# Two transformer blocks on one core: the embedding stage ends tile by tile, and block 2 opens without a row norm stage

## What is computed

```python
def first_block(x, p, ...):
    for i in range(DEPTH):
        h = rms_norm(x, g_mix[i])
        ...
        x = x + merged @ w_out[i]
        x = x + expert_choice_moe(rms_norm(x, g_moe[i]), ...)
        ple_gate = jax.nn.sigmoid(rms_norm(x, g_ple[i]) @ w_ple_gate[i])
        x = x + ple_gate * (p[i] @ w_ple[i])
    return rms_norm(x, g_final)

def second_block(x, c, norm_g, w_ada, ...):
    for l in range(DEPTH):
        h = hybrid_layer(h, c_silu, cos, sin, norm_g[l], ...)
    return rms_norm_2(h, final_g)
```

## Time and profile before

| | us |
|---|---|
| median of 3 runs (3681.97 to 3682.17) | 3681.98 |
| the profiled execution's own time | 3682.63 |
| its span, first to last instruction | 3680.9 |
| PE busy in the span | 3421.2 (93%) |
| DVE busy | 1760.2 (48%) |
| ACT busy | 1064.4 (29%) |
| POOL busy | 38.6 (1%) |

### The profile page before, as it was taken

How to read it: one execution, slowest core, us unless ns; L and a number is a source line. 1 busy time by engine, 2 the same in 40 slices (tenths; PEclk the granted TensorE clock), 3 DMA queues, 4 the chain that set the end, 5 groups by cost and what they waited for, 6 DMA issues and landing times. The chain is left out here.

```text
span 3680.9 us, 41926 instructions
## 1 busy us (share of the span) xinstructions
PE 3421.2 (93%) x16364; PEld 2281.5 (62%) x16364; DVE 1760.2 (48%) x3023; ACT 1064.4 (29%) x1684; POOL 38.6 (1%) x42
## 2 busy tenths in 40 slices
PE   7999996999988999996999997999999999999999
PEld 5866673444446866675444445777766687777666
DVE  7766633212135875744121224467654355666443
ACT  4343322101023334322011013343333234433322
POOL 1000000000000200000000000000000000000000
PEclk9999998999998999997999998999999999999999
DMA  5521127999963441124999982212321331222213
GB/s 191 193 94 58 58 86 310 423 423 424 424 250 129 157 144 58 58 94 189 420 424 424 423 351 71 93 61 66 92 81 69 106 115 58 68 76 86 69 69 115
DMA packets 129376, 653.28 MB, mean 177 GB/s; under 512 B 22036, under 2 KB 32276, under 8 KB 62136
## 3 DMA queue, kind: packets, MB, share of 16 engines
q1 hardware_dynamic: 129208, 650.98, 45.6%
HBM read 632.54 MB, written 14.72 MB: 176 GB/s over the span
## 5 line engine op out<-in xcount | busy, mean ns | idle before, releaser
L1733 PE MATMUL ps<-normed_T_hi,ring_split 128*128 128x512 f32 x1920 | 609.8, 399 | 7.5 <-PEq L264 7.5
L1733 PEld LDWEIGHTS ps<-normed_T_hi,ring_split 128*128 128x128 f32 x1920 | 354.5, 188 | 107.4 <-issue 34.3
L1733 PE MATMUL ps<-normed_T_lo,ring_split 128*128 128x512 f32 (+1 forms) x960 | 376.1, 392 | 0.0
L2486 PE MATMUL ps<-normed_T_hi,ring_split 128*128 128x512 f32 x1024 | 336.1, 410 | 8.9 <-DVE branches L2752 7.6
L2065 DVE TENSOR_TENSOR ring_split<-weight_ring,ring_split 128x2048 fp32r<-128x2048 f32 x76 | 174.0, 2289 | 151.9 <-ACT ring_split L1921 151.6
L2486 PEld LDWEIGHTS ps<-normed_T_hi,ring_split 128*128 128x128 f32 x1024 | 192.9, 192 | 81.6 <-issue 32.7
L1733 PEld LDWEIGHTS ps<-normed_T_lo,ring_split 128*128 128x128 f32 (+1 forms) x960 | 180.2, 188 | 40.0
L2486 PE MATMUL ps<-normed_T_lo,ring_split 128*128 128x512 f32 x512 | 202.6, 396 | 0.0
L1789 PE MATMUL ps<-branches 128*128 128x512 f32 x384 | 173.0, 593 | 3.3 <-issue 3.0
L1230 PE MATMUL ps<-weight_ring,projected 128*64 128x512 f32 x768 | 167.9, 593 | 0.0
L1921 ACT ACTIVATE ring_split<-weight_ring 128x2048 fp32r<-128x2048 f32 x76 | 144.9, 1912 | 52.5 <-DMA weight_ring<-in_w_slabs 48.1
(11 more groups left out here) (443 smaller groups left out, 6028.3 us busy)
## 6 DMA issues: line engine op xcount, KB each, us to landing
weight_ring<-in_w_slabs SPq DMA_DIRECT2D x78, 1024.0 KB, 4.9
weight_ring<-in_w_exp_gate SPq DMA_DIRECT2D x48, 1024.0 KB, 16.9
weight_ring<-in_w_exp_down SPq DMA_DIRECT2D x48, 1024.0 KB, 12.2
weight_ring<-in_w_exp_up SPq DMA_DIRECT2D x48, 1024.0 KB, 20.5
weight_ring<-in_w_branch_gate SPq DMA_DIRECT2D x32, 1024.0 KB, 4.9
spare_weights<-in_w_exp_up SPq DMA_DIRECT2D x32, 1024.0 KB, 21.0
spare_weights<-in_w_exp_gate SPq DMA_DIRECT2D x32, 1024.0 KB, 20.3
spare_weights<-in_w_exp_down SPq DMA_DIRECT2D x32, 1024.0 KB, 15.7
```

Source lines behind the costliest of these rows:

```text
L1733: ins = e.matmul(dst, lhs(k, m), rhs(k, m), start=k == 0 and m == 0, stop=k == KD - 1 and m == 2)
L2486: ins = e.matmul(dst, lhs(k, m), rhs(k, m), start=k == 0 and m == 0, stop=k == KD - 1 and m == 2)
```

## The change

In `embedding_stage`, PE now does kh = 0 of tile 0, then the side products, then kh = 1 of tile 0, and for tiles 1 to 3 both halves of the depth one after the other; so tiles end one by one. ACT adds up the squares of each finished tile there (`squares`), and in the last layer DVE also writes `gained_X` = `X` times the gain of `g_final`, and ACT adds up its squares too. SP loads the first slab of the next stage in this stage, and ACT and DVE split it ahead of the stage that uses it. The norm stage ahead of layer 1's front (`summed`) then has no squares, no load and no split of slab 0. `row_norm_stage` and the norm stage behind it are gone: both roots come from the two sums (the second norm's variance is m2/(v+eps)+eps, with m2 the mean square of the gained row, which is worked out as eps*(v+eps)+m2 for the product of both roots). `layer2_stage(0)` is called with "summed" and opens by itself: four small DVE operations, one root, one reciprocal, three tiles scaled by DVE and one by ACT, 32 transposes, and steps 0 and 1 in halves of 256 tokens. POOL writes the normed `X` itself, four tiles of 128x1024; SP saves each tile to DRAM when POOL has written it, and SP and DVE wait for the four stores before they go on.

```diff
-        def norm_stage(loads, scale_col, bias_col=None, experts_of=None, save=False, slabs=None, ple=None):
+        def norm_stage(loads, scale_col, bias_col=None, experts_of=None, save=False, slabs=None, ple=None, summed=False):
...
-                        for q in range(3):
+                        for q in range(int(summed), 3):
...
+                    if summed:
+                        e.tensor_tensor(sums[:, 3, 0:1], sums[:, 3, 0:1], sums[:, 4, 0:1], ALU.add).then_inc(s["vector_step"], st.add("vector_step"))
+                        e.wait_ge(s[st.name], st.value)
+                        e.tensor_scalar(var, sums[:, 0:4, 0], 1.0 / D, EPS, ALU.mult, ALU.add).then_inc(s["var_ready"], 1)
...
 def embedding_stage(l):
...
                 @block.sync
...
+                            if last_layer:
+                                e.dma_start(rope_T[:, :, :], a["c_rope_T"]).then_inc(s["inputs_loaded"], 16)
+                                e.dma_start(gain_row, a["g_final"].partition_broadcast(P)).then_inc(s["inputs_loaded"], 16)
+                                e.dma_start(small[:, 136:152], modulation_saved[0, :, :]).then_inc(s["inputs_loaded"], 16)
+                    e.wait_ge(s["lo_ready"], 2)
+                    e.dma_start(ring_land[:, 0, :], next_slab).then_inc(slot_loaded[0], 16)
...
                 @block.tensor
...
+                    e.wait_ge(s["lo_ready"], 2)
+                    e.wait_ge(s["exp_done"], 1)
+                    exact_products(e, PS[:, 0, :], 0, 0, 0, 512)
+                    e.wait_ge(s["side_landed"], 16)
+                    for t in range(NT):
+                        e.wait_ge(s["gate_used"], t + 1)
+                        for k in range(2):
+                            ins = e.matmul(PS[:, 4 + t, :], p_T[:, k, t * P:(t + 1) * P], ple_side[:, k, :], start=k == 0, stop=k == 1)
+                        ins.then_inc(s["side_ready"], 1)
+                    e.wait_ge(s["lo_ready"], 3)
+                    for t in range(NT):
+                        if t:
+                            exact_products(e, PS[:, t, :], t, 0, 0, 512)
+                        exact_products(e, PS[:, t, :], t, 1, 1, 512).then_inc(s["product_ready"], 1)
...
                 @block.scalar
...
+                    e.wait_ge(slot_loaded[0], EXPERT_LOADS + 32)
+                    e.wait_ge(s["lo_ready"], 3)
+                    e.activation(ring_hi[:, 0, :], ring_land[:, 0, :], ACT.Copy).then_inc(s["slab_hi"], 1)
+                    sigmoid(1, 0)
+                    squares(0, 0, whole, 5, 1)
+                    sigmoid(1, 1)
+                    squares(1, 1, whole, 6, 2)
+                    squares(3, 4, low, 4, 3)
+                    sigmoid(1, 2)
+                    squares(2, 2, whole, 7, 4)
+                    sigmoid(1, 3)
+                    e.preload_act_table(ACT.Sqrt)
+                    squares(3, 3, high, 8, 5)
...
-        def layer2_stage(l, turned_by_last):
+        def layer2_stage(l, begun):
...
                 @block.sync
...
+                        for q in (1, 2):
+                            e.dma_start(ring_land[:, q, :], a["w_slabs_2"][l, q, :, :]).then_inc(slot_loaded[q], 16)
+                        for t in range(NT):
+                            e.wait_ge(s["pool_ready"], t + 1)
+                            e.dma_start(x_saved[t * P:(t + 1) * P, :], X[:, t, :]).then_inc(s["stored"], 16)
+                    e.wait_ge(s["stored"], 16 if half_turned else 64)
...
                 @block.tensor
...
+                        e.wait_ge(s["scaled_by_vector"], 1)
+                        turn_tile(e, s, U, open_banks, 0, lambda pair: None)
+                        e.wait_ge(s["scaled_by_scalar"], 1)
+                        turn_tile(e, s, U, open_banks, 1, None)
+                        e.wait_ge(s["scaled_by_vector"], 2)
+                        turn_tile(e, s, U, open_banks, 2, lambda pair: e.wait_ge(s["turned_taken_scalar"], 2 * pair - 2) if pair >= 2 else None)
+                        e.wait_ge(s["scaled_by_vector"], 3)
+                        turn_tile(e, s, U, open_banks, 3, None)
+                        half_step(0, 0, lambda k: k + 1)
+                        half_step(1, 0, lambda k: 8)
+                        half_step(0, 1, lambda k: k + 9)
+                        half_step(1, 1, lambda k: 16)
...
+                @block.gpsimd
...
+                        e.wait_ge(s["rstd_ready"], 1)
+                        for t in range(NT):
+                            e.tensor_scalar(X[:, t, :], gained_X[:, t, :], open_rstd[:, t:t + 1], None, ALU.mult).then_inc(s["pool_ready"], 1)
...
                 @block.scalar
...
+                        e.activation(U[:, 1, :], gained_X[:, 1, :], ACT.Copy, scale=open_rstd[:, 5:6]).then_inc(s["scaled_by_scalar"], 1)
+                        take_turned(e, s, open_banks, 0, 2, range(KD), lambda k: 0)
+                        take_turned(e, s, open_banks, 1, 4, range(KD), lambda k: k + 1)
...
                 @block.vector
...
+                        for t in (0, 2, 3):
+                            e.tensor_scalar(U[:, t, :], gained_X[:, t, :], open_rstd[:, 4 + t:5 + t], None, ALU.mult).then_inc(s["scaled_by_vector"], 1)
+                        split_taken(e, s, 0, range(KD), 0, st_)
+                        split_taken(e, s, 1, range(KD), 8, st_)
+                        e.wait_ge(s["stored"], 64)
...
-        row_norm_stage("g_final")
-        norm_stage([(modulation_cols, modulation_saved[0, :, :])], scale_col2, shift_col, save=True, slabs=lambda q: a["w_slabs_2"][0, q, :, :])
         for l in range(DEPTH):
-            layer2_stage(l, l > 0)
+            layer2_stage(l, "half turned" if l else "summed")
```

More of the change, by code:

```diff
@@ L1047, in _, with gain @@
+                    def gain(t, cols, done):
+                        if last_layer:
+                            e.wait_ge(tile_done, done)
+                            e.tensor_tensor(gained_X[:, t, cols], X[:, t, cols], gain_row[:, cols], ALU.mult).then_inc(gained, 1)
                     split(1, 1)
                     split(2, 0)
-                    add(0)
+                    for t in range(NT):
+                        add(0, t)
                     split(3, 1)
-                    add(1)
@@ L1052, in _ @@
[L1052 removed]
+                    e.wait_ge(s["slab_hi"], 1)
+                    e.tensor_tensor(ring_lo[:, 0, :], ring_land[:, 0, :], ring_hi[:, 0, :].bitcast(F32), ALU.subtract).then_inc(s["slab_lo"], 1)
+                    if last_layer:
+                        e.wait_ge(s["inputs_loaded"], 48)
+                    add(1, 0)
+                    gain(0, whole, 5)
+                    add(1, 1)
+                    gain(1, whole, 6)
+                    gain(3, low, 4)
@@ L1055, in mixer_kernel @@
+                    add(1, 2)
+                    gain(2, whole, 7)
+                    add(1, 3)
+                    gain(3, high, 8)
+                    e.wait_ge(tile_done, 8)
         chosen = T[:, 3072:3584].rearrange("p (t n) -> p t n", t=NT)
@@ L1325, in mixer_kernel @@
         half_var = small[:, 16:17]
+        open_var, open_root, open_rstd = (small[:, 8 * i:8 * i + 8] for i in range(3))
         final_gain, squares2 = T[:, 2048:3072], T[:, 3072:4096]
```

291 lines of the change are left out of this document (151 added, 140 removed).

## The result

The changed kernel takes 3650.4 us (median of four runs, 3648.6 to 3657.7) against 3682.0: a ratio of 0.992 with an interval of 0.990 to 0.994. The profiled execution took 3652.1, its span is 3650.0, 30.9 less than the span of before.

The account below looks back on a forecast made before the run. PE is busy 93% of the span, so time is won at two handovers where it waits on an ACT and DVE chain. Gains of 6.4 and 18.9 sum to 25.3 us, giving 3657; range 3651 to 3664.

Parts of the forecast that it names:

- The first handover: Embedding 0 to layer 1's front: scaling 3.1 us earlier and slab 0's split gone from the end, 3.3; together 6.4 us.
- The embedding's cover: Embedding, side products after one tile's 12 matmuls: 1.3 us to spare, no stall, PE ends at the old place.
- Rival 3: Embedding loses its cover: about 2 us in each of two stages, 3661; chance 0.07 together with rival 5.
- The second handover: Embedding 1 to block 2's opening: step 2 starts at 2304.4 instead of 2323.3, a gain of 18.9 us.
- I take 1.6: Block 2's opening: POOL's time in us to scale one tile of X, chosen between bounds of 1.04 and 2.1.
- I let each DVE operation wait for the POOL operation that is under way: Block 2's opening: POOL holds DVE for whole operations, and the reverse; DVE's pieces of half 1 end at 2301.1.
- rival 2: Block 2's opening: POOL takes 3.0 us per tile, step 2 at 2309.9, total 3662; chance 0.13.
- PE follows the last piece by 0.4 and has one half step left: End of block 2's opening: the half step left takes 2.9 us after DVE's last piece, so step 2 starts at 2304.4.
- A shift of step 2 is a shift of all that follows: From block 2's step 2 on, the program is the same in both kernels, so the gain there is kept whole.
- Rival 5: Behind block 2's opening: a later wait takes the shift back, a few us, 3660; chance 0.07 together with rival 3.
- Rival 1: Block 2's opening: POOL doesn't hold DVE up or is at its lower bound; step 2 at 2301.7, total 3653; chance 0.20.
- Rival 4: Block 2's opening: the four stores of X hold DVE; slower from 10.5 us per POOL tile, 3692 at 13; chance 0.02.

Follow-up runs that it names:

- second profile: The changed kernel run again without an edit: median 3650.7 us over five runs, its profiled execution 3655.3 us.
- pool_eighth: Against the changed kernel, GpSimd scales only the first 128 of 1024 columns of each tile of X; 3649.7 us in one run.
- pool_twice: Against the changed kernel, GpSimd scales each tile of X twice over; 3664.3 us in one run.
- split_behind: Against the changed kernel, slab 0's split for layer 1's front goes back to the end of the norm stage; 3657.0 us in one run.

## Why the prediction was right, and where it was off

- **The first handover** held by its own steps. The scaling came 3.2 us earlier (3.1 forecast), the removed split gave 3.3. The two microseconds of clock that were left to the range did not come in the first profile; in the second the front's first dense product is 2 us earlier for it (+20.72 instead of +22.68).
- **The embedding's cover** held: the 16 side matmuls run from 2243.60 to 2250.07, 6.5 us (6.6 forecast), with no gap behind, and from the front to the embedding's end it is 1112.5 us against 1112.7. Rival 3 is out.
- **The second handover**, against the embedding's last matmul: scaling +5.3 (5.4 forecast), first piece +9.8 (9.5), ACT's last piece done +20.9 (20.4), DVE's last split +21.7 (24.3), step 2 +26.3 (27.6). The first three steps stand. The fourth failed twice, in opposite directions: "I take 1.6" for POOL's tile was half of the 3.07 measured, and "I let each DVE operation wait for the POOL operation that is under way" is refuted: with POOL's work doubled, DVE's splits ended 1.5 us later, since a DVE operation waits for a part of a POOL operation only (last section). With the price right and the wait as assumed, rival 2's 3662 would have come out; with both wrong the sum was 1.3 us from the truth. That it came out near is luck in this term.
- **The end of the chain** was PE and not DVE: "PE follows the last piece by 0.4 and has one half step left" put 3.3 us between the last split and step 2; it was 4.7, since PE had 96 half matmuls to do from its own start on. That is why POOL's slowing cost nothing in the opening that pool_eighth can be compared with, and at most the 1 us of PE's waits in the changed kernel.
- **"A shift of step 2 is a shift of all that follows"** is the step that missed the total. 26.7 us at the handovers against the 25.3 of the sum is an error of 1.4; the other 4 us of the first profile lie outside the handovers, 1.6 of them in TensorE's clock behind step 2 and 1.1 behind the last matmul, which the sum took as the same in both. In the second profile the step held (1358.0 us behind step 2 against 1357.6). That the medians lie as low as the first profile is in keeping with the clocks of the runs, but no trace of those runs shows it. Rival 5 did not come: from 1352.0 to 1358.0 us lie behind step 2 in the changed kernels, against 1357.6, so that no later wait took the shift back.
- **The rivals.** Rival 1 gave the nearest number (3653) and half of the reason: POOL delays step 2 by 1 us at most, but not for a low price. The Trainium skill (GPSIMD Engine Reference, Engine selection), which has one-input elementwise work on GpSimd at roughly line rate, would have 1.1 us a tile as an estimate; the trace has 3.07, so here page and measurement differ. By the prediction's own steps, four tiles of 1.1 instead of 1.6 would have lowered its sum by 2.0 us and not by the 1.5 that it gives. Rival 4's mechanism exists: at 6.0 us per tile, as in pool_twice, the stores cost 8.1 us; each further microsecond per tile would add four, so the other 18.6 of the 26.7 us need 4.65 more. As an estimate that is 10.7 us per tile, where the prediction put the turning point at 10.5.

## What to carry to other kernels

Cost a handover from the last product of the stage before, and look for what ends last among all engines in it: the price of a helper engine is hidden as long as another engine has more left to do, and comes back as soon as that one is made faster. Where TensorE waited some 6 us ahead of short work here, that work ran at half its clock, and for how long differed between executions; matmuls into a free bank took that out, worth 1.0 to 2.9 us up to the front's first dense product. And a difference of two spans should be split at marks before it is explained: in the first profile here 4 of 31 us lay outside the stretches that the change touches.

## What was not expected of the hardware

- GpSimd's scaling of 128x1024 took 3.76 us for the first tile and 2.84 to 2.88 for those behind it; of 128 columns 1.61 for the first and 0.60 for the last two. Beside it DVE's casts of 128x256 grew from 0.29 to between 0.28 and 1.15 us, but none took as long as an operation of GpSimd.
- DVE was not slowed evenly: it was held in two parts of each of GpSimd's operations. In the changed kernel a subtraction that started 0.2 us behind the start of a GpSimd tile ended 1.4 us behind that start (1.22 us instead of 0.43), and a cast that started in a tile's last 0.6 us ended 0.15 us behind the tile's end; casts that started 1.7 us behind a tile's start took their own 0.28, subtractions from 1.3 us on their own 0.42.
- ScalarE started its table load 0.44 us behind its last work, ahead of the wait of the root that needs it, so that the late load of 1.28 us brought the transposes only 0.87 us later at the first handover, and 0.56 at the second against split_behind, where ACT's last square started 0.3 us late as it did here.
- TensorE's granted clock after an idle time of 6.1 us came back to 1.00 some 10 us behind the last product in one execution, and after 6.4 us 19 us behind it in another of the same instructions.
